# A streaming encoder layer on one core: prompt z and gate projections as fills between attention steps, expert search in quarters, old keys in 1 KB rows

## What is computed

```python
proj = jnp.einsum('bld,de->ble', x, w_in)             # D = 1024
q, k, v, qi, ki, wi, z, xbc_raw, dt_raw, gate_pre = jnp.split(proj, offs, axis=-1)
q, k, qi, ki = partial_rope(...)                      # z has 2048 columns, gate_pre 2048
score = einsum(relu(qi . ki), wi); sel = lax.top_k(score, k_sel)      # indexer
attn  = softmax(q . k[sel] / 8) @ v[sel]              # 16 heads, 4 key/value heads
xbc   = silu(causal_conv(xbc_raw, conv_prev))         # 3072 channels, width 4
y_ssm = rmsnorm(ssd(xbc, softplus(dt_raw + dt_bias)) * silu(z)) * norm_w
gates = sigmoid(gate_pre + b_gate)
mix   = (gates[0] * (attn @ w_attn_br) + gates[1] * (y_ssm @ w_ssm_br)) @ w_out
h     = layer_norm(ALPHA * x + mix)
# PEER: per token 8 heads, each the 16 best of 128 x 128 experts
q = h @ peer_wq;  s1 = q[..., :128] @ keys1.T;  s2 = q[..., 128:] @ keys2.T
v1, i1 = top_k(s1, 16);  v2, i2 = top_k(s2, 16)
top_s, top_i = top_k(v1[:, None] + v2[None, :], 16);  expert = i1 * 128 + i2
act = gelu(h . peer_u[expert]);  out = sum(softmax(top_s) * act * peer_v[expert])
y   = layer_norm(ALPHA * h + out)
```

## Time and profile before

| | |
|---|---|
| median of 3 runs | 1923.47 us (1921.11 to 1931.13) |
| profiled execution: time, span | 1929.03 us, 1927.2 us |
| mean granted TensorE clock | 0.863 of full |
| PE busy | 1476.2 us (77%) |
| DVE busy | 1071.4 us (56%) |
| POOL busy | 837.6 us (43%) |
| ACT busy | 436.0 us (23%) |
| moved | 625.16 MB, mean 324 GB/s |
| first expert gather | 437.9 us |

### The profile page before, as it was taken

The page is one execution under the profiler, slowest core; times in us unless marked ns, Lnnn a source line. Parts: engine busy times, 40 slices in busy tenths (PEclk is TensorE's granted clock), DMA queues, the critical chain, the costliest instruction groups (busy, mean ns, idle before and its releaser), DMA issues.

```text
span 1927.2 us, 20577 instructions
## 1 busy us (share of the span) xinstructions
PE 1476.2 (77%) x7481; PEld 696.1 (36%) x7481; DVE 1071.4 (56%) x2722; ACT 436.0 (23%) x1083; POOL 837.6 (43%) x776
## 2 busy tenths in 40 slices
PE   8989898898995678788779895787688745555654
PEld 7544565357442224333356332334233311111111
DVE  3422386156473556824766646648833878755454
ACT  1111423011103243321211114333311211221111
POOL 0000000004303776735634205776735657777774
PEclk9989878999998688889989997789898967677678
DMA  9976354769996999999999986999999979999997
GB/s 307 309 230 202 115 164 145 259 195 383 398 322 224 344 363 373 374 353 401 389 344 402 393 274 225 346 373 347 340 368 402 367 259 376 407 403 407 403 406 283
DMA packets 251909, 625.16 MB, mean 324 GB/s; under 512 B 21892, under 2 KB 58948, under 8 KB 251624
## 3 DMA queue, kind: packets, MB, share of 16 engines
q0 software_dynamic: 110736, 402.88, 54.9%
q1 hardware_dynamic: 141072, 220.96, 33.5%
HBM read 611.55 MB, written 12.23 MB: 324 GB/s over the span
## 4 chain that ended last, share of the span: by engine, by line
PE 44%; POOL 17%; DMA 14%; DVE 13%; issue 7%; ACT 4%; SPq 0%; POOLq 0%; DVEq 0%; ACTq 0%
PE bank L617 24%; POOL BIG L537 17%; DMA wbuf<-in_w_in_dram 7%; DMA BIG<-in_peer_v_dram,BIG 7%; PE bank L574 7%; PE bank L680 5%; DVE BIG L1345 3%; ACT BIG L1025 3%; PE bank L657 3%; ACT L1025 1%; DVE BIG L1612 1%; PE bank L903 1%; DVE BIG L1584 1%; PE bank L626 1%; DVE BIG L1600 0%
## 5 line engine op out<-in xcount | busy, mean ns | idle before, releaser
L537 POOL DMA_INDIRECT BIG<-in_peer_u_dram,BIG x384 | 422.3, 1100 | 851.5 <-DVEq L1739 473.9
L574 PE MATMUL bank<-BIG 64*64 64x512 f32 x3072 | 500.7, 767 | 293.2 <-DMA BIG<-in_peer_v_dram,BIG 222.2
L617 PE MATMUL bank<-wbuf,BIG 128*128 128x512 f32 x1152 | 522.5, 610 | 27.0 <-DMA wbuf<-in_w_in_dram 22.8
L1345 DVE CUSTOM_DVE_ANT_0 BIG<-BIG 128x1024 f32<-128x1024 f32 x384 | 459.3, 1222 | 121.1 <-DMA BIG<-in_peer_u_dram,BIG 118.5
L537 POOL DMA_INDIRECT BIG<-in_peer_v_dram,BIG x384 | 412.4, 1074 | 216.7 <-PE bank L574 112.9
L574 PEld LDWEIGHTS bank<-BIG 64*64 64x64 f32 x3072 | 113.4, 156 | 627.2 <-issue 381.7
L617 PEld LDWEIGHTS bank<-wbuf,BIG 128*128 128x128 f32 x1152 | 219.6, 195 | 324.8 <-issue 301.2
L1025 ACT ACTIVATE BIG<-bank 128x512 f32<-128x512 f32 (+5 forms) x231 | 117.8, 539 | 669.0 <-PE bank L617 342.9
L1025 ACT ACTIVATE BIG<-cst,small 128x64 f32<-128x64 f32 x384 | 112.1, 339 | 359.7 <-DVE small L1340 359.7
L657 PE MATMUL bank<-cst,BIG 128*128 128x128 f32 (+3 forms) x551 | 97.6, 333 | 70.2 <-ACT BIG L1025 24.0
L680 PE MATMUL bank<-BIG,wbuf 128*128 128x128 f32 x1152 | 136.7, 282 | 14.8 <-DMA wbuf<-in_w_in_dram 13.3
(11 more groups left out here) (159 smaller groups left out, 951.7 us busy)
## 6 DMA issues: line engine op xcount, KB each, us to landing
wbuf<-in_w_in_dram SPq DMA_DIRECT2D x108, 1024.0 KB, 8.5
wbuf<-in_w_ssm_br_dram SPq DMA_DIRECT2D x24, 1024.0 KB, 6.5
wbuf<-in_peer_wq_dram SPq DMA_DIRECT2D x24, 1024.0 KB, 12.8
wbuf<-in_w_attn_br_dram SPq DMA_DIRECT2D x12, 1024.0 KB, 5.0
wbuf<-in_w_out_dram SPq DMA_DIRECT2D x12, 1024.0 KB, 10.4
BIG<-in_state_ssm_dram SPq DMA_DIRECT2D x16, 512.0 KB, 6.5
out_s_ssm_dram<-BIG SPq DMA_DIRECT2D x16, 512.0 KB, 3.8
BIG<-in_peer_u_dram,BIG POOLq DMA_INDIRECT x384
```

The source lines that it names most:

```text
L537: pool.indirect_dma_start(slot, None, table, bass.IndirectOffsetOnAxis(ap=eidx[:, col:col + 1], axis=0)).then_inc(done, 16)
L574: last = mm(acc[i][64 * half:64 * half + 64, :], dg[rows, :], vslot[k][rows, 512 * half:512 * half + 512], start=False, stop=False, skip_g ...
L617: last = mm(dst[:, :], lhs[:, HALF * h + k, :], w[:, k, :], start=(first and h + k == 0), stop=(end and h == 1 and k == HALF - 1))
L1345: nc.vector.tensor_tensor_reduce(uslot[s], uslot[s], H[k // BLOCKS], 1.0, 0.0, ALU.mult, ALU.add, dots[k % 2][:, j:j + 1]).then_inc(dot_do ...
```

## The change

- **z and gates in passes 1 and 2** no longer stand behind q/k/v. All three passes now do them as fills: one ahead of the place `tails`, one ahead of `keys`, one between the two `select` places, and one behind `item2` of each of the five items. They go to ACT's two banks in all passes; the banks 6 and 7, the table `FILL_AT` and the two semaphores are gone from this use. SP waits for a fill's number in ACT's ring (`filled_at`) to free a weight buffer.
- **Places.** `gates` and `dt` are gone; `z` has one tick at each of four places, `select` 1 + 1 instead of 2 + 1, `seg` one each instead of 2, 1, 2, 1. DVE has the `z` ticks inside its convolution. In pass 0 the `late` places can now hold ticks.
- **ACT's order.** Time steps and the Silu of the convolution come ahead of the fills; `glu` comes behind the attention in every pass.
- **Search in quarters** of two heads. Part 0 runs ahead of the first four `late` places; then the limit rises by 16 blocks, and part 1 runs with the last four; parts 2 and 3 run at the `conv` and `qkv` places of the next pass. POOL waits for a part before each 16 blocks.
- **Old keys** come in one DMA with rows of 1 KB (all four heads of a position), and PE transposes them with 40 matmuls against the identity, 64 columns each, one for each stream.
- SP stores a pass's new keys and values ahead of its third z tile in every pass (before in passes 1 and 2 behind the weights of `w_attn_br`).

```diff
-FILLS = 8
-FILL_AT = dict(dt=(2,), keys=(1,), item1=(1,), item2=(1, 0))
-TICKS_AT = dict(dt=(0,), z=(0,), gates=(0,), select=(2, 1), xbt=(2,), seg=(2, 1), y=(2, 1), late=(2, 1), last=(2,))
+PARTS = 4
+PART = BLOCKS // PARTS
+TICKS_AT = dict(xbt=(2,), y=(2, 1), late=(2, 1), last=(2,))
...
+        def filled_at(q, j):
+            at = before[q.n, "attention"][1]
+            if j == 0:
+                return at
+            at += 2 + 5 * q.streams
+            return at + j if j < 3 else at + j + 2 * max(0, j - 4) + max(0, j - 5)
...
@@ SP: old keys, z and gates, new rows
-                    for v in range(KVH):
-                        sp.dma_start(q.kc[:, v, :].rearrange("p (b n) -> p b n", b=DEC_B),
-                                     a["cache_k"][0][:, :, v, :].rearrange("b s n -> s b n")).then_inc(cache_in, 16)
...
+                    sp.dma_start(q.kc, a["cache_k"][0].rearrange("b s v n -> s b (v n)")).then_inc(cache_in, 16)
+                    sp.dma_start(q.kic, a["cache_kidx"][0].rearrange("b s n -> s b n")).then_inc(cache_in, 16)
...
                 for j in range(8):
-                    if q.first and j == 2:
-                        for c in range(SOON):
-                            old_state(c)
+                    if j == 2:
+                        if q.first:
+                            for c in range(SOON):
+                                old_state(c)
                         store_new_rows(q)
                     load(wtile(w_in, O_Z + 512 * j if j < 4 else O_GATE + 512 * (j - 4)),
-                         (fill_done, j + 1) if q.first else (sb_filled, at["z"][1] + j + 1))
+                         (sb_filled, filled_at(q, j)))
...
-                if not q.first:
-                    store_new_rows(q)
...
@@ POOL
-                    if b % (BLOCKS // 2) == 0:
-                        pool.wait_ge(idx_ready, b // (BLOCKS // 2) + 1)
+                    if b % PART == 0:
+                        pool.wait_ge(idx_ready, b // PART + 1)
...
@@ PE, mixer
-                phase("z")
-                if not q.first:
-                    for j in range(8):
-                        sf.give(in_tile(sbank(), j))
-                        step("z" if j < 4 else "gates")
-                step("dt")
+                for _ in range(4):
+                    step("z")
+                gate_tiles = iter(range(8))
+
+                def fill():
+                    sf.give(in_tile(sbank(), next(gate_tiles)))
...
+                fill()
                 step("tails")
...
                         for j in range(4):
-                            last = turn(dst[:, j * P:(j + 1) * P], q.kc[:, v, j * P:(j + 1) * P], ident)
+                            for half in range(2):
+                                src = q.kic[:, 2 * j + half, :] if v == KVH else q.kc[:, 2 * j + half, v * HD:(v + 1) * HD]
+                                last = mm(dst[64 * half:64 * half + 64, j * P:(j + 1) * P], src, ident, start=True, stop=True)
...
+                fill()
                 step("keys")
...
                     if v == KVH:
                         step("select")
+                        fill()
                         step("select")
...
                     step("item2")
+                    fill()
                     if last_kv:
                         times_values(items[m - 1])
...
-                step("late")
-                step("late")
+                steps.at("late")
+                steps.limit = q.n * BLOCKS + PART
+                steps.at("late")
                 if q.n + 1 < TILES:
                     x_to_T(passes[q.n + 1])
...
@@ ACT, mixer
+                for _ in range(4):
+                    step("z")
+                time_steps()
+                gate_tiles = iter(range(8))
+
+                def fill():
+                    src = bank()
+                    sd.give(f(kept(next(gate_tiles)), src[:, :]))
...
                 keep_heads(items[-1])
-                if q.first:
-                    glu()
+                sd.upto(act)
+                glu()
...
+                exp_scores(q.n, 0)
+                steps.at("late")
+                steps.limit = q.n * BLOCKS + PART
+                steps.at("late")
...
                     if i == 2:
-                        exp_scores(q.n, 0)
-                    step("late")
+                        exp_scores(q.n, 1)
+                    steps.at("late")
...
@@ DVE
-                    pick(q.n - 1, 1, lambda place: step("conv" if place < CONVS - EARLY else "qkv"))
+                    pick(q.n - 1, 2, lambda: step("conv"))
+                    pick(q.n - 1, 3, lambda: step("qkv"))
...
-                pick(q.n, 0, lambda place: step("late"))
+                pick(q.n, 0, lambda: steps.at("late"))
+                steps.limit = q.n * BLOCKS + PART
+                pick(q.n, 1, lambda: steps.at("late"))
```

More of the change, by code:

```diff
@@ L126, in tick_places @@
     return TICKS_AT.get(place, (1,))
-def fill_places(place):
-    return FILL_AT.get(place, (0,))
 class Count:
@@ L443, in _ @@
                 n = q.n
-                at = {name: before[n, name] for name in ("conv", "qkv", "z", "ya", "ym", "out", "wq")}
+                at = {name: before[n, name] for name in ("conv", "qkv", "ya", "ym", "out", "wq")}
                 for i in range(CONVS):
@@ L686, in mixer @@
             def mixer(q):
-                t = q.t
-                step = fills.at if q.first else steps.at
+                t, step = q.t, steps.at
                 def phase(name):
@@ L1090, in mixer @@
                     conv_tile(q, i)
+                    if i == CONVS - 1 and not q.first:
+                        exp_scores(q.n - 1, 2)
                     step("conv")
@@ L1097, in mixer, with time_steps @@
                     if j == 3 and not q.first:
-                        exp_scores(q.n - 1, 1)
+                        exp_scores(q.n - 1, 3)
                     step("qkv")
-                if not q.first:
-                    for j in range(8):
-                        src = bank()
-                        sd.give(f(kept(j), src[:, :]))
-                        step("z" if j < 4 else "gates")
-                act.wait_ge(dt_v, 2 * q.n + 1)
-                if q.first:
-                    f(negA, headp[:, SH:2 * SH], ACT.Exp)
-                f(dtu, dta, ACT.Exp, scale=-1.0).then_inc(dt_e, 1)
-                act.wait_ge(dt_v, 2 * q.n + 2)
-                f(dtw, dtw, ACT.Ln).then_inc(dt_e, 1)
+                def time_steps():
+                    act.wait_ge(dt_v, 2 * q.n + 1)
+                    if q.first:
+                        f(negA, headp[:, SH:2 * SH], ACT.Exp)
+                    f(dtu, dta, ACT.Exp, scale=-1.0).then_inc(dt_e, 1)
+                    act.wait_ge(dt_v, 2 * q.n + 2)
+                    f(dtw, dtw, ACT.Ln).then_inc(dt_e, 1)
+                    act.wait_ge(conv_done, CC * (q.n + 1))
+                    f(C, C, ACT.Silu).then_inc(silu_done, 1)
                 def glu():
@@ L1115, in glu @@
                     f(GX, GX, ACT.Sigmoid).then_inc(gates_ready, 1)
-                act.wait_ge(conv_done, CC * (q.n + 1))
-                f(C, C, ACT.Silu).then_inc(silu_done, 1)
-                if not q.first:
-                    glu()
-                step("dt")
+                for _ in range(4):
[5 more added lines that the diff above has]
+                    sd.give(f(kept(next(gate_tiles)), src[:, :]))
                 if t != 0:
@@ L1424, in mixer @@
                 if q.first:
-                    for _ in range(4):
-                        step("qkv")
-                else:
-                    for _ in range(4):
-                        step("gates")
-                step("dt")
+                    for place in ("conv",) * (CONVS - EARLY) + ("qkv",) * 4 + ("z",) * 4:
+                        step(place)
                 dve.wait_ge(par_in, 48)
@@ L1759, in _ @@
             dve.wait_ge(sb_drained, SR + before[2, "end"][1])
-            pick(2, 1, lambda place: steps.at("last"))
+            for part in (2, 3):
+                pick(2, part, lambda: steps.at("last"))
             places.append(list(steps.seen))
```

100 lines of the change are left out of this document (39 added, 61 removed).

## The result

The changed kernel takes 1907.96 us (median; 1903.40 to 1909.29) where the kernel before took 1927.3 beside it (1921.11 to 1933.19): a ratio of 0.9896, 95% interval [0.9856, 0.9936]. That is 20 us less, not 84, and 8 us above the range. The profiled execution took 1908.5 us with a span of 1906.7.

A forecast was written before the change was run, and what follows sets the result against it. Bound taken: 531 MB of memory traffic from the first expert gather on, plus stretches where queues run dry. Terms -33 - 37 - 8 - 9 + 6 - 3 = -84 us from 1929.0 gave 1845 us, range 1800 to 1900.

The forecast's parts named there:

- z and gates as fills, -33 and -37: From q/k/v's end to the attention's end in passes 1 and 2: filled queues gain 33 and 37 us.
- I take 376, the row of 719 to 919: Rate in GB/s assumed for that whole stretch, from a window mixing weights, ticks and dependent steps: 156 and 157 us.
- The serial rival: Attention: fills add themselves to the items instead of slipping into waits; 36 us an item gives 1969 us, chance 0.07.
- 20 us from the other parts: Gain from parts other than the fills, credited when working out the item time at which fills in series break even.
- break-even: Attention item time at which fills in series neither gain nor lose: 32 us, against 21.7 us in the kernel before.
- half the gain: Convolution stage starves PE and the queue as much as the attention gains: 1870 to 1912 us, chance 0.13.
- Its sign: Mark of a wrong forecast, in the convolution: PE idle for 30 us with the DMA share below 0.8.
- Search in quarters, -8, -9 and +6: Earlier first gather gains 8 us, shorter search wait ending pass 2 gains 9, extra small DVE instructions lose 6.
- the wait at the end of pass 2: POOL's 13.7 us wait for the search there: a shorter search saves 9 us, leaving it below 5 us.
- Old keys and the sample pass, -3: Fewer old-key issues and weight waits, against more narrow matmuls and fills waiting for ACT's ring: 3 us gained.
- Memory gives no more: 357 GB/s is all this mix yields over a pass, so only the earlier first gather gains: 1918 us, chance 0.05.

The follow-up runs named there:

- taps_before: Kernel before with three of the four taps of the prompt passes' convolution left out: 1931.53 us, 1.0004 of the kernel before.
- taps_after: Changed kernel with three of the four taps of the prompt passes' convolution left out: 1843.55 us, 0.9574 of the kernel before.
- f_only: Changed kernel with the search put back into halves, so fills and old keys alone: 1906.82 us, 0.9853 of the kernel before.
- z_fill: Changed kernel with five of eight z and gate tiles placed earlier in all three passes, three left in the attention: 1914.56 us, 0.9912 of the kernel before.
- zp2_raise2: Changed kernel, prompt passes' z and gate tiles earlier, three ticks a pass fewer in the scan, limit raised in the last pass alone: 1861.52 us, 0.9653 of before.

## Why the prediction was wrong

The sign was right, the size was not: 20 us for 84.

- **z and gates as fills, -33 and -37.** The step that failed is "I take 376, the row of 719 to 919", one rate for the whole stretch: 156 and 157 us from the end of q/k/v to the end of the attention. It took 193 us at 351 GB/s and 207 at 328, longer than before (with 23 ticks in it, by the tables of places, where before had 20). The attention did what was forecast: items of (746.1 - 622.9) / 5 = 24.7 us in pass 1 and 25.2 in pass 2 with a tile in each, 391 and 395 GB/s, POOL's waits of 68 us gone (the longest for a dot product is 15.6). The part ahead of it got 233 and 223 GB/s. I had read z and gates as work that keeps the queues from gathers, and had not asked what they cover: 34 us of DVE's convolution (24 chunks of 1.42 us) and its rotation, which nothing else covered. taps_before and taps_after show it: the same DVE work costs nothing before and is fully on the path after. The serial rival's working had this time: 48 us of convolution, rotation and ticks, three fills and five items, which at 24.7 us an item end at 617 + 123 = 740 (measured 746); the sum did not use it. (Its "20 us from the other parts" leave out the 6 us lost; with 14 its break-even is 31 us an item, not 32.) f_only, fills and old keys together, is 1.5% under before, some 28 us, where the sum had 73. By f_only's columns the fills won 36 us ahead of the attention, gave 41 back in it, and the scan's stretches won 10: 5.5 us net from S0 to S2 in that profile.
- **The rival "half the gain"** (the convolution starves PE and the queue; 1870 to 1912, chance 0.13) is what happened, at its weak end: 1908. Its sign was written down as well, PE idle for 30 us in the convolution with a DMA share below 0.8: it stood 26 of 50 us at 0.67 in pass 1 and 39.6 of 54 in pass 2, where the share was 0.63 from 1104 to 1185. Its price lay in my own reading: DVE takes 38 us for convolution and rotation, and what I put beside them, four ticks of about 2 us of PE each and one tile ahead of the rotation's end, leaves most of that uncovered.
- **Search in quarters, -8, -9 and +6.** Measured: nothing that shows (0.9995, by its interval 7 us at most; and halves against quarters the same with the tiles placed well). The first gather did come earlier and PE's convolution did wait 10.9 us, as written. What failed is to count an earlier gather as time won. Each of the six ticks that it lets in costs 4 to 6 us of DVE's and PE's order beside the search, about what it would cost in the tail. Nor did the wait at the end of pass 2 vanish: four ticks stood beside that search, as forecast, but POOL issues ahead of the ticks and had issued the last of their gathers by 1526.6, 16.7 us before the search was done.
- **Old keys and the sample pass, -3.** Not tried alone. The issue of the old keys fell from 5.46 to 0.51 us, but the loads behind it took longer: from the first of them to the next weights SP's queue took 8.3 us against 9.9. The column up to S0 is 395 to 405 with the new layout (z_fill aside) and 403 to 411 with the old. That agrees with some microseconds and shows no more.
- **"Memory gives no more".** Rightly given little: the mean from the first gather on rose from 357 to 369 GB/s in zp2_raise2, and to 376 over 1418 us in taps_after. The Trainium skill's figure of about 358 GB/s for one core (DMA: Bandwidth & Descriptors, Specifications), quoted in the forecast, is there worked out as half of what a stack has for two cores. The Trainium skill says elsewhere (Perfetto Trace Analysis, Roofline) that a core can pull more than that while the other is idle. These runs, on one core, agree with the second; none had another core at work.

## What to carry to other kernels

Before work is moved away from a place, list what runs beside it on the other engines and how long that is: it comes onto the path when the cover goes. Move only as much as leaves the cover whole (here five of eight tiles stay in the fastest kernels; other numbers were not tried), and fill the place that is emptied. Starting a queue earlier is no gain where the same engines must serve it: cut the span at fixed marks and see whether the later stretch shrinks by more than the earlier one grows.

## What was not expected of the hardware

A tick's 16 matmul records took 1.95 us where PE came from other work (at 1107.07), and 3.34 to 3.69 us where it had stood idle for 7.4 to 7.9 us (1116.91 to 1138.94; the rows are in the close-up). In the windows the granted clock is 0.64 of full speed from 1115 to 1140, a mean over the two levels of 1.2 and 2.4 GHz, and 1.00 from 1165 on, when PE had tiles again. In the 5 us that hold the first slow tick it is 0.54, close to the lower level:

```profile
1116.00:1121.00 5.00, 3.69 (x16) 0.80 (x16) 4.81 (x13) 0.79 (x3) 2.75 (x3) 0.54 0.22 48
```

So the hole also made its own few matmuls nearly twice as long, some 5 us a pass, but in pass 2 off the path: behind them PE waits again for ACT, 7.4, 7.6 and 16.7 us.
